# Semaphores of a finished phase cleared one phase later: one barrier between phases in place of two

## The chip, the core and the metric

The kernel runs on one NeuronCore of a Trainium2 chip. The core has five engines that run side by side, each through its own list of instructions: TensorE (PE, with its weight loads as PEld), VectorE (DVE), ScalarE (ACT), GpSimd (POOL) and SyncE (SP, which here only issues DMAs). They are kept in order by semaphores: an instruction adds to one when it ends, another engine waits until it has reached a number. Sixteen DMA engines move data between memory and the core's buffers. The metric is the time of one execution on the device in microseconds; the median of several runs counts.

## The reference

One layer of a hybrid network is computed for 128 context tokens and 512 latent tokens, 640 rows of 1024 numbers:

```python
def layer(x, mod, init_f, init_b, ctx_k, ctx_v, pos, lp):
    shift1, scale1, gate1, shift2, scale2, gate2 = jnp.split(mod, 6, axis=-1)
    h = modulate(rmsnorm(x, lp['norm1_w']), shift1, scale1)
    mix, s_f, s_b, k, v = token_mixer(h, init_f, init_b, ctx_k, ctx_v, pos, lp)
    x = x + gate1 * mix
    h = modulate(rmsnorm(x, lp['norm2_w']), shift2, scale2)
    x = x + gate2 * peer(h, lp['w_pq'], lp['peer_keys'], lp['peer_u'], lp['peer_v'])
    return x, s_f, s_b, k, v
```

token_mixer projects h once, runs a state-space scan in both directions (ssd_scan) and grouped attention beside each other, and merges both with sigmoid gates. peer picks for each token and each of 8 heads the best 16 of 16384 single-neuron experts by two lists of 128 keys, and sums gate * gelu(x.u) * v over them. The change touches none of this arithmetic.

## The kernel before

The work is cut into ten phases that follow each other: modulate, tokens, attention, attn_out, ssd, ssd_out, mix_out, route, gates and experts. `build` (line 2565) calls `run_phase` for each. A phase allocates its buffers and semaphores, and then opens one `nc.Block()` with a function for every engine that has work in it: `block.sync` issues DMAs, `block.tensor`, `block.vector`, `block.scalar` and `block.gpsimd` hold the instructions of the four compute engines. Inside a phase the order is that of the code, engine by engine, with semaphores between them. A block ends with a barrier: every engine drains, reports to POOL and goes on when POOL releases it.

All phases use the same numbers of semaphores again, and each phase counts from zero. So `run_phase` opens a second block behind each phase (lines 2558 to 2562), in which POOL clears that phase's semaphores one by one, and which ends with a barrier of its own. The phases have 36, 40, 19, 6, 48, 21, 16, 25, 8 and 31 semaphores, 250 in all. In the profile line 2562 is the clear, and line 2558 the barrier behind the clears.

Weights come as a stream of units of 1 MB (`Stream`, line 87): SP loads a unit into one of two buffers (`load`, L98), ACT rounds it to its upper part (`hi`, L106), DVE makes the remainder (`lo`, L111), and PE multiplies with both. The stream's semaphores, the two for the gate matrix (`K.g_out`) and the eight for gathered rows (`K.gathered`) belong to no phase and are never cleared. Loads for the first units of a phase are issued in the phase before it; a phase's own parameters are loaded by SP at its start.

Two places matter besides. The gates phase (line 2100) builds a matrix of gate weights and writes it to memory in blocks, the last of them as `g_late` (L2130). The experts phase (line 2194) begins on SP and on POOL with the wait for all of these writes; then SP loads pieces of the matrix (`p_g`, L2247 and L2249), and POOL issues 256 indirect DMAs (L2308) that gather rows of u and v into `p_uv`, while PE, ACT and DVE run all experts over the other tokens. `K.pool_dma_sems` (line 2574) are twelve more semaphores that no instruction uses.

Of the kernel before, what the change touches and what calls it, by code (L numbers as in the profile page):

```python
# [27 lines left out]
NT = T // P  # L28
# [278 lines left out]
def phase_tokens(nc, K, ctx):  # L307

    S = Stream(nc, K)
    sem = K.phase_semaphores(ctx)  # L310
# [53 lines left out]
    with nc.Block() as block:  # L364
# [47 lines left out]
        @block.gpsimd  # L412
        def _(pool):
            nc.gpsimd.memset(b_row[:, :], 0.0).then_inc(brow_zero, 1)
            pool.wait_ge(nrm_in, 48)
            for n, w in enumerate((wq, wk)):
                for f in range(2):
                    part = w[:, :].rearrange("p (a f d) -> p a f d", a=2, f=2)[:, :, f, :].unsqueeze(1).to_broadcast([P, 4, 2, 16])
                    for j in range(2):
                        nc.gpsimd.tensor_tensor(rope[:, n, f, j], cs[:, j, :, :].rearrange("p t (a d) -> p t a d", a=2), part,  # L420
                                                ALU.mult).then_inc(tab_done, 1)

        @block.scalar
        def _(act):
# [249 lines left out]
def phase_attention(nc, K, ctx):  # L674

    S = Stream(nc, K)
    sem = K.phase_semaphores(ctx)
# [52 lines left out]
    with nc.Block() as block:  # L730
# [12 lines left out]
        @block.gpsimd  # L743
        def _(pool):
            nc.gpsimd.memset(cin[:, :, :], 0.0).then_inc(zero, 1)

        @block.tensor
        def _(pe):
# [167 lines left out]
def phase_attn_out(nc, K, ctx):  # L916
    S = Stream(nc, K)
    sem = K.phase_semaphores(ctx)
    sb = lambda n, s, d=F32: ctx.enter_context(nc.sbuf_tensor(n, s, d))
    oT = [sb(f"g_oT{i}", [P, KD, T], F32R) for i in range(2)]  # L920
    yb = [sb(f"g_yb{i}", [P, 4, TH]) for i in range(2)]
    ps = [[ctx.enter_context(nc.psum_tensor(f"g_ps{s}{i}", [P, TH], F32)) for i in range(4)] for s in range(2)]
    oh_done = sem("g_oh"); ol_done = sem("g_ol"); mm_done = sem("g_mm"); ev_done = sem("g_ev")
    out_done = [sem("g_out0"), sem("g_out1")]

    with nc.Block() as block:
        @block.sync
        def _(sp):
            for i in range(N_AT):
                S.load(sp, U_AT + i + 3, (i + 1) % 2)  # L930
                sp.wait_ge(ev_done, 4 * (i + 1))
                sp.dma_start(K.yb_dram[2 * i:2 * i + 2].rearrange("m p t -> p m t"),
                             yb[i % 2][:, :, :].rearrange("p (m a) t -> p m (a t)", a=2)).then_inc(out_done[i % 2], 16)
            for s in range(2):
                sp.wait_ge(out_done[s], 16 * N_AT // 2)

        @block.tensor
        def _(pe):
            for i in range(N_AT):
                s = i % 2  # L940
                S.ready(pe, U_AT + i)
                if i >= 2:
                    pe.wait_ge(ev_done, 4 * (i - 1))
                wh, wl = (x[s][:, :].rearrange("p (k c) -> p k c", k=KD) for x in (K.whi, K.wlo))
                for m in range(2):
                    for k in range(KD):
                        if i == 0 and m == 0 and k % 2 == 0:
                            pe.wait_ge(ol_done, k // 2 + 1)
                        cols = slice(m * P, (m + 1) * P)
                        for lhs, rhs, f, l in ((wh, oT[0], k == 0, False), (wh, oT[1], False, False), (wl, oT[0], False, k == KD - 1)):  # L950
                            for h in range(2):
                                mm = nc.tensor.matmul(ps[s][2 * m + h][:, :], lhs[:, k, cols], rhs[:, k, h * TH:(h + 1) * TH],
                                                      start=f, stop=l)
                mm.then_inc(mm_done, 1)
                pe.drain().then_inc(K.hilo_free, 1)

        @block.scalar
        def _(act):
            for q in range(4):
                nc.scalar.activation(oT[0][:, 2 * q:2 * q + 2, :], K.QT[:, 2 * q:2 * q + 2, :], ACT.Copy).then_inc(oh_done, 1)  # L960
            for i in range(N_AT):
                act.wait_ge(mm_done, i + 1)
                if i >= 2:
                    act.wait_ge(out_done[i % 2], 16)
                for b in range(4):
                    nc.scalar.activation(yb[i % 2][:, b, :], ps[i % 2][b][:, :], ACT.Copy).then_inc(ev_done, 1)
                S.hi(act, U_AT + i + 2, i % 2)

        @block.vector
        def _(dve):  # L970
            for q in range(4):
                dve.wait_ge(oh_done, q + 1)
                nc.vector.tensor_tensor(oT[1][:, 2 * q:2 * q + 2, :], K.QT[:, 2 * q:2 * q + 2, :],
                                        oT[0][:, 2 * q:2 * q + 2, :].bitcast(F32), ALU.subtract).then_inc(ol_done, 1)
            for i in range(N_AT):
                S.lo(dve, U_AT + i + 2, i % 2)
# [4 lines left out]
def phase_ssd(nc, K, ctx):  # L981

    S = Stream(nc, K)
    sem = K.phase_semaphores(ctx)
# [72 lines left out]
    with nc.Block() as block:  # L1057
# [63 lines left out]
        def _(pool):  # L1121
# [45 lines left out]
            for q in range(SLOTQ):  # L1167
                a, b, f = ssd_steps(q)
                g, k = (q - 2) // NT, (q - 2) % NT
                if 0 <= g < GROUPS:  # L1170
                    carry(g, k)
                    if k == 4:
                        carry(g, 5)
                if b is not None:
                    forward_part(b)
                if q >= NT - 1 and q - NT + 1 < STEPS:
                    build_rT(q - NT + 1)
                if b is not None:
                    skip(b)

        @block.tensor
        def _(pe):
# [264 lines left out]
def phase_ssd_out(nc, K, ctx):  # L1447
# [30 lines left out]
    with nc.Block() as block:  # L1478
# [97 lines left out]
        @block.gpsimd  # L1576
        def _(pool):
            pool.wait_ge(row_done, 2)
            for c in range(4):
                pool.wait_ge(sig_done, 2 * c + 2)  # L1580
                nc.gpsimd.tensor_tensor(ga[c % 2][:, :, :], ga[c % 2][:, :, :], rrow[:, :].unsqueeze(1).to_broadcast([P, 2, T]),
                                        ALU.mult).then_inc(scaled, 1)

        @block.scalar
        def _(act):
# [66 lines left out]
def phase_mix_out(nc, K, ctx):  # L1652
# [20 lines left out]
    with nc.Block() as block:  # L1673
        @block.sync
        def _(sp):
            sp.dma_start(x[:, :, :], K.x.rearrange("(t p) d -> p t d", p=P)).then_inc(x_in, 16)
            for g in range(2):
                sp.dma_start(g1[:, g, :], K.gates[g:g + 1, 0:D].partition_broadcast(P).rearrange("p o d -> p (o d)")).then_inc(x_in, 16)
            for n in range(U_O, U_PQ):
                S.load(sp, n + 3, (n + 3) % 2)  # L1680
            for t in range(NT):
                sp.wait_ge(res, NT + t + 1)
                sp.dma_start(K.x2_dram[t * P:(t + 1) * P, :], x[:, t, :]).then_inc(x_out, 16)
                sp.wait_ge(x_out, 16 * (t + 1))

        @block.tensor
        def _(pe):
# [120 lines left out]
def phase_route(nc, K, ctx):  # L1808
# [50 lines left out]
    with nc.Block() as block:  # L1859
# [9 lines left out]
        def _(pool):  # L1869
            for h in range(LOOKED_UP):  # L1870
# [5 lines left out]
                for i, n in enumerate((8 * TOPK, 4 * TOPK, 2 * TOPK)):  # L1876
# [3 lines left out]
                nc.gpsimd.tensor_tensor(slots[:, 0:2, :, TOPK * h:TOPK * (h + 1)], pair[:, :, :, 0:TOPK], pair[:, :, :, TOPK:2 * TOPK],  # L1880
                                        ALU.add).then_inc(x_done, 1)
                pool.wait_ge(x_done, h + 1)

        @block.tensor
        def _(pe):
# [214 lines left out]
def phase_gates(nc, K, ctx):  # L2100
# [20 lines left out]
    with nc.Block() as block:  # L2121
# [23 lines left out]
        @block.gpsimd  # L2145
        def _(pool):
            for g in range(ALL):
                pool.wait_ge(hot_done, 2 * g + 1)
                nc.gpsimd.tensor_tensor(oi[g % HOT][:, :, :], oi[g % HOT][:, :, :],
                                        K.slotsT[:, 2, Q * g:Q * (g + 1)].unsqueeze(2).to_broadcast([P, Q, P]), ALU.mult).then_inc(weighted, 1)  # L2150

        @block.tensor
        def _(pe):
# [40 lines left out]
def phase_experts(nc, K, ctx):  # L2194
# [43 lines left out]
    with nc.Block() as block:  # L2238
# [62 lines left out]
        def _(pool):  # L2301
# [10 lines left out]
            nc.gpsimd.tensor_tensor(ys[:, 0, :], ys[:, 0, :], gate2[:, group(0), :], ALU.mult).then_inc(gated0, 1)  # L2312
            pool.wait_ge(gated0, 1)
            nc.gpsimd.tensor_tensor(res[0], res[0], ys[:, 0, :], ALU.add).then_inc(summed0, 1)

        @block.tensor
        def _(pe):
# [222 lines left out]

def run_phase(nc, K, phase):

    K.sems = []

    def phase_semaphores(ctx):
        def sem(name):
            K.sems.append(ctx.enter_context(nc.semaphore(name)))
            return K.sems[-1]
        return sem

    def pool_dma(i):

        return K.pool_dma_sems[i]

    K.phase_semaphores, K.pool_dma = phase_semaphores, pool_dma
    with ExitStack() as ctx:
        phase(nc, K, ctx)
        with nc.Block() as block:  # L2558
            @block.gpsimd
            def _(pool):  # L2560
                for s in K.sems:
                    pool.sem_clear(s)


def build(nc, K):
    ctx = ExitStack()
    with ctx:
# [3 lines left out]
        K.whi = [sb(f"w_hi{i}", [P, 8 * UC], F32R) for i in range(2)]  # L2571
        K.wlo = [sb(f"w_lo{i}", [P, 8 * UC], F32R) for i in range(2)]
        K.w_loaded = [sem("w_loaded0"), sem("w_loaded1")]
        K.pool_dma_sems = [sem(f"pool_dma{i}") for i in range(NT + 7)]
        K.w_hi_done, K.w_lo_done, K.hilo_free = (sem(n) for n in ("w_hi_done", "w_lo_done", "hilo_free"))
        K.ident, K.ones, K.iota = sb("ident", [P, P]), sb("ones", [P, P]), sb("iota", [P, P])
        K.tri_le, K.tri_gt, K.tri_ge, K.tri_lt = (sb(n, [P, P]) for n in ("tri_le", "tri_gt", "tri_ge", "tri_lt"))
# [29 lines left out]
        with ExitStack() as s:  # L2607
# [4 lines left out]
            for phase in (phase_route, phase_gates):  # L2612
                run_phase(nc, K, phase)
        run_phase(nc, K, phase_experts)


def pack_units(w, cols=UC):
# [71 lines left out]
```

## Time and profile before

| | us |
|---|---|
| median of 3 runs | 2834.81 |
| fastest and slowest run | 2831.0 and 2839.09 |
| span of the profiled execution | 2836.8 |

The page gives one time for the profiled execution, its span from the first instruction to the last; the runs' median is 2.0 us below it. Of the span PE is busy 2575.1 us, DVE 2142.1, ACT 1135.1 and POOL 864.4. Clears, barriers and other semaphore instructions are not counted as busy, so a stretch in which a core only clears semaphores reads as idle on all engines. Names such as POOLq or SPq mean an engine's instruction queue: what it did outside its compute unit. Line numbers are those of the kernel before.

### The profile page before, as it was taken

Reading aid. Unit: us, or ns where it says so; the run is one execution under the profiler, and the core shown is the slowest. Engines: PE = TensorE matmul, PEld = TensorE weight load, DVE = VectorE, ACT = ScalarE, POOL = GpSimd, SP = SyncE. Lnnn points to the kernel's source line nnn. Section 1 sums busy time; section 2 is a strip of 40 time slices with the busy share of each in tenths; the row PEclk is TensorE's granted clock in tenths of the full one; section 3 lists DMA queues with packets and bytes.
Section 4 is the critical chain, followed back from the end, with each engine's and each line's share of the span. In section 5 each row is a group of like instructions: output and inputs, shape, how many; then the busy total and the mean of one; then the engine's idle time right before and its main releaser. Section 6 shows DMA issues by size and latency. Waiting matters only on the chain. (4 is left out here: it accounts for less than half of the span.)

```text
span 2836.8 us, 39212 instructions
## 1 busy us (share of the span) xinstructions
PE 2575.1 (91%) x14998; PEld 2227.3 (79%) x14998; DVE 2142.1 (76%) x3785; ACT 1135.1 (40%) x1882; POOL 864.4 (30%) x623
## 2 busy tenths in 40 slices
PE   5979999978899999698799988899999999999996
PEld 3868777768788787598688668788888888888885
DVE  2646667661478777433489978699999999999998
ACT  3324445442465565332334467233333323333332
POOL 0000000000466666110023356343433443334431
PEclk9989999989999999799799999899999999999998
DMA  5521112122223222342312338999999999999995
GB/s 227 223 110 49 49 64 82 51 95 104 105 75 129 96 80 84 104 178 97 126 51 76 112 115 250 401 417 416 418 414 417 418 413 417 413 412 419 411 410 232
DMA packets 166265, 621.49 MB, mean 219 GB/s; under 512 B 14880, under 2 KB 83264, under 8 KB 105664
## 3 DMA queue, kind: packets, MB, share of 16 engines
q1 hardware_dynamic: 124608, 340.03, 32.2%
q0 software_dynamic: 36864, 268.45, 23.0%
q10 hardware_dynamic: 4608, 10.52, 1.2%
q8 instruction: 119, 1.95, 0.3%
q14 instruction: 66, 0.54, 0.1%
HBM read 559.39 MB, written 59.56 MB: 218 GB/s over the span
## 5 line engine op out<-in xcount | busy, mean ns | idle before, releaser
L2308 POOL DMA_INDIRECT p_uv<-in_uv_rows,merged x256 | 395.6, 1545 | 625.1 <-DVE merged L2475 564.7
L2475 DVE SCALAR_TENSOR_TENSOR merged<-p_uv,p_sw,merged 128x1024 f32<-128x1024 f32 x256 | 330.9, 1292 | 7.5 <-DVE p_sw L2465 0.4
L2328 PE MATMUL p_pa<-h2D,w_hi 128*128 128x384 f32 x896 | 318.2, 355 | 3.0 <-PEq L2558 2.2
L2458 DVE CUSTOM_DVE_ANT_0 p_uv<-p_uv,merged 128x1024 f32<-128x1024 f32 x256 | 308.0, 1219 | 16.7 <-DMA p_uv<-in_uv_rows,merged 16.7
L2330 PE MATMUL p_pa<-h2D,w_lo 128*128 128x384 f32 x896 | 301.9, 337 | 0.0
L2329 PE MATMUL p_pa<-h2D,w_hi 128*128 128x384 f32 x896 | 301.8, 337 | 0.0
L2343 PE MATMUL p_py<-w_hi,p_wh 128*128 128x512 f32 x672 | 267.6, 398 | 15.0 <-DVE w_lo L2429 15.0
L2372 ACT ACTIVATE w_hi<-w_raw 128x2048 fp32r<-128x2048 f32 x110 | 210.4, 1913 | 173.8 <-DMA w_raw<-in_w_stream 88.6
L2429 DVE TENSOR_TENSOR w_lo<-w_raw,w_hi 128x2048 fp32r<-128x2048 f32 x110 | 251.8, 2289 | 22.7 <-ACT w_hi L2372 22.6
L2344 PE MATMUL p_py<-w_lo,p_wh 128*128 128x512 f32 x672 | 266.7, 397 | 0.0
L2345 PE MATMUL p_py<-w_hi,p_wl 128*128 128x512 f32 x672 | 266.7, 397 | 0.0
L111 DVE TENSOR_TENSOR w_lo<-w_raw,w_hi 128x2048 fp32r<-128x2048 f32 x64 | 153.2, 2395 | 102.3 <-ACT w_hi L106 102.3
L1145 POOL TENSOR_TENSOR s_pv<-s_pv,decay 128x256 f32<-128x256 f32 x48 | 41.1, 856 | 536.8 <-ACT s_st L1306 535.6
L801 PE MATMUL c_pp<-hT,w_hi 128*128 128x320 f32 x1024 | 199.1, 317 | 0.0
L2328 PEld LDWEIGHTS p_pa<-h2D,w_hi 128*128 128x128 f32 x896 | 169.0, 189 | 14.0 <-issue 12.0
L2329 PEld LDWEIGHTS p_pa<-h2D,w_hi 128*128 128x128 f32 x896 | 169.1, 189 | 10.0 <-issue 9.6
L2330 PEld LDWEIGHTS p_pa<-h2D,w_lo 128*128 128x128 f32 x896 | 168.9, 189 | 0.0
L106 ACT ACTIVATE w_hi<-w_raw 128x2048 fp32r<-128x2048 f32 x64 | 122.5, 1914 | 112.5 <-PEq L1574 68.5
L2343 PEld LDWEIGHTS p_py<-w_hi,p_wh 128*128 128x128 f32 x672 | 127.0, 189 | 45.9 <-DVE w_lo L2429 17.4
L801 PEld LDWEIGHTS c_pp<-hT,w_hi 128*128 128x128 f32 x1024 | 161.6, 191 | 0.3
L853 DVE TENSOR_REDUCE a_nmax<-a_ps 128x1 f32<-128x640 f32 (+1 forms) x80 | 57.4, 717 | 130.5 <-PE a_ps L759 112.7
L2345 PEld LDWEIGHTS p_py<-w_hi,p_wl 128*128 128x128 f32 x672 | 127.0, 189 | 30.9
(379 smaller groups left out, 6271.5 us busy)
## 6 DMA issues: line engine op xcount, KB each, us to landing
w_raw<-in_w_stream SPq DMA_DIRECT2D x174, 1024.0 KB, 9.1
g_pairs<-e_st SPq DMA_DIRECT2D x5, 4096.0 KB, 16.1
p_g<-g_pairs SPq DMA_DIRECT2D x64, 320.0 KB, 8.4
t_ada<-in_w_ada SPq DMA_DIRECT2D x16, 1024.0 KB, 10.3
xc_dram<-c_xc SPq DMA_DIRECT2D x8, 1284.0 KB, 4.5
p_ve<-in_v_early SPq DMA_DIRECT2D x8, 1024.0 KB, 13.5
r_ur<-in_u_early ACTq DMA_DIRECT2D x14, 512.0 KB, 3.6
s_xx<-xc_dram SPq DMA_DIRECT2D x8, 642.0 KB, 6.0
```

The costliest lines, as they stand in the source:

```text
L801: mm = nc.tensor.matmul(ps_p[:, h, 0:TH], lhs[:, k, cols], rhs[:, k, h * TH:(h + 1) * TH], start=f, stop=l)
L2308: nc.gpsimd.indirect_dma_start(uv[:, k % RING, :], None, K.uv_rows, bass.IndirectOffsetOnAxis(K.sidx[:, t, c:c + 1], 0)).then_inc(K.gather ...
L2328: nc.tensor.matmul(ps_a[m][:, :], wh[:, k, cols], K.h2D[0][:, k, :], start=k == 0, stop=False)
L2329: nc.tensor.matmul(ps_a[m][:, :], wh[:, k, cols], K.h2D[1][:, k, :], start=False, stop=False)
L2330: mm = nc.tensor.matmul(ps_a[m][:, :], wl[:, k, cols], K.h2D[0][:, k, :], start=False, stop=k == KD - 1)
L2343: nc.tensor.matmul(ps_y[o][:, :], Wh[s][:, c, tc], vh[:, c, dc], start=first and c == 0, stop=False)
L2344: nc.tensor.matmul(ps_y[o][:, :], Wh[s][:, c, tc], vl[:, c, dc], start=False, stop=False)
L2345: mm = nc.tensor.matmul(ps_y[o][:, :], Wl[s][:, c, tc], vh[:, c, dc], start=False, stop=last and c == 1)
L2372: nc.scalar.activation(K.whi[slot][:, :], K.raw[slot][:, :], ACT.Copy).then_inc(K.w_hi_done, 1)
L2429: nc.vector.tensor_tensor(K.wlo[slot][:, :], K.raw[slot][:, :], K.whi[slot][:, :].bitcast(F32), ALU.subtract).then_inc(K.w_lo_done, 1)
L2458: nc.vector.tensor_tensor_reduce(uv[:, b, 0:D], uv[:, b, 0:D], K.hrow[:, t, :], 1.0, 0.0, ALU.mult, ALU.add, sa[:, at:at + 1]).then_inc(do ...
L2475: nc.vector.scalar_tensor_tensor(ys[:, t, :], uv[:, b, D:2 * D], sw[:, at:at + 1], ys[:, t, :], ALU.mult, ALU.add).then_inc(v_done, 1)
```

## The change

The clears move into the next phase. `run_phase` no longer opens a block of its own. Every phase ends its POOL function with `K.clear_previous(pool)`, which clears the semaphores of the phase before it; phases that had no POOL function (attn_out, mix_out) get one that holds only this. Since a phase's semaphores now live until the next phase is over, two sets are held at a time, and the numbers of a set are free again for the phase after the next. The twelve unused semaphores are dropped. The last phase's 31 semaphores are not cleared any more.

```diff
@@ phase_tokens, and likewise at the end of POOL's function in attention, ssd, ssd_out, route, gates, experts
                         nc.gpsimd.tensor_tensor(rope[:, n, f, j], cs[:, j, :, :].rearrange("p t (a d) -> p t a d", a=2), part,
                                                 ALU.mult).then_inc(tab_done, 1)
+            K.clear_previous(pool)
@@ phase_attn_out, and likewise mix_out
+        @block.gpsimd
+        def _(pool):
+            K.clear_previous(pool)
@@ run_phase
-    K.sems = []
+    sem_ctx, sems = ExitStack(), []
 
     def phase_semaphores(ctx):
         def sem(name):
-            K.sems.append(ctx.enter_context(nc.semaphore(name)))
-            return K.sems[-1]
+            sems.append(sem_ctx.enter_context(nc.semaphore(name)))
+            return sems[-1]
         return sem
 
-    def pool_dma(i):
-
-        return K.pool_dma_sems[i]
-
-    K.phase_semaphores, K.pool_dma = phase_semaphores, pool_dma
+    def clear_previous(pool):
+
+        for s in K.previous_sems:
+            pool.sem_clear(s)
+
+    K.phase_semaphores, K.clear_previous = phase_semaphores, clear_previous
     with ExitStack() as ctx:
         phase(nc, K, ctx)
-        with nc.Block() as block:
-            @block.gpsimd
-            def _(pool):
-                for s in K.sems:
-                    pool.sem_clear(s)
+    K.previous_ctx.close()
+    K.previous_ctx, K.previous_sems = sem_ctx, sems
@@ build
-        K.pool_dma_sems = [sem(f"pool_dma{i}") for i in range(NT + 7)]
+        K.previous_ctx, K.previous_sems = ExitStack(), []
...
         run_phase(nc, K, phase_experts)
+        K.previous_ctx.close()
```

On POOL at the handover from modulate to tokens (ISA is a clear; the branches open and close blocks; `tri_lt` and `iota` are modulate's last work, `q_brow` and `q_rope` tokens' own) the difference of the two orders reads:

```order
 L189 IOTA iota 128x128
 L160 UNCONDITIONAL_BRANCH
-L2559 UNCONDITIONAL_BRANCH
-L2562 ISA x36
-L2558 UNCONDITIONAL_BRANCH
 L412 UNCONDITIONAL_BRANCH
 L414 MEMSET q_brow 128x512
 L420 TENSOR_TENSOR q_rope<-q_cs,q_w 128x128 x4
 L420 TENSOR_TENSOR q_rope<-q_cs,k_w 128x128 x4
+L2569 ISA x36
 L364 UNCONDITIONAL_BRANCH
```

The 36 clears went from between the two phases to behind tokens' last tensor instruction, and one block with its barrier is gone.

On POOL at the end of the program, before, from the end of the gates phase (`h`) through the experts phase (`p_uv`, `merged`):

```order
L2149 TENSOR_TENSOR h<-h,slotsT 128x1024 x48
L2121 UNCONDITIONAL_BRANCH
L2559 UNCONDITIONAL_BRANCH
L2562 ISA x8
L2558 UNCONDITIONAL_BRANCH
L2300 UNCONDITIONAL_BRANCH
L2308 DMA p_uv<-in_uv_rows,merged 128x2048 x256
L2312 TENSOR_TENSOR merged<-merged,w_raw 128x1024
L2314 TENSOR_TENSOR merged<-merged 128x1024
L2238 UNCONDITIONAL_BRANCH
L2559 UNCONDITIONAL_BRANCH
L2562 ISA x31
```

and of the changed kernel, the same stretch (line numbers are 12 to 14 higher there):

```order
L2162 TENSOR_TENSOR h<-h,slotsT 128x1024 x48
L2569 ISA x25
L2134 UNCONDITIONAL_BRANCH
L2314 UNCONDITIONAL_BRANCH
L2322 DMA p_uv<-in_uv_rows,merged 128x2048 x256
L2326 TENSOR_TENSOR merged<-merged,w_raw 128x1024
L2328 TENSOR_TENSOR merged<-merged 128x1024
L2569 ISA x8
L2252 UNCONDITIONAL_BRANCH
```

The clears of route (25) now stand behind POOL's last work in gates, those of gates (8) behind its last work in experts, and the 31 at the end are gone. On PE, ACT, DVE and SP the order of the instructions is as before but for the second barrier's.

## Rows read from the trace of the kernel before

**Rows 1.** The page's part 1: busy us (share of the span) xinstructions, by engine.

```profile
PE 2575.1 (91%) x14998; PEld 2227.3 (79%) x14998; DVE 2142.1 (76%) x3785; ACT 1135.1 (40%) x1882; POOL 864.4 (30%) x623
```

**Rows 2.** Stretches: us from:to, length, busy us of each engine (xinstructions), PEclk, DMA share, GB/s.

```profile
1770.30:2834.30 1064.00, 1026.37 (x4896) 884.65 (x4896) 1002.66 (x1201) 331.57 (x406) 400.90 (x258) 0.98 0.99 403
```

**Rows 3.** Stretches, same columns: from first clear to release, nine handovers and the end.

```profile
57.00:59.70 2.70, 0.00 (x0) 0.00 (x0) 0.00 (x0) 0.00 (x0) 0.00 (x0) 0.50 0.19 79
191.00:194.10 3.10, 0.00 (x0) 0.00 (x0) 0.00 (x0) 0.00 (x0) 0.00 (x0) 0.50 0.00 0
631.30:632.80 1.50, 0.00 (x0) 0.00 (x0) 0.00 (x0) 0.00 (x0) 0.00 (x0) 0.50 0.00 0
701.70:702.30 0.60, 0.00 (x0) 0.00 (x0) 0.00 (x0) 0.00 (x0) 0.00 (x0) 0.50 0.00 0
1165.00:1168.60 3.60, 0.00 (x0) 0.00 (x0) 0.00 (x0) 0.00 (x0) 0.00 (x0) 0.50 0.00 0
1311.00:1313.00 2.00, 0.00 (x0) 0.00 (x0) 0.00 (x0) 0.00 (x0) 0.00 (x0) 0.50 0.02 4
1404.90:1406.20 1.30, 0.00 (x0) 0.00 (x0) 0.00 (x0) 0.00 (x0) 0.00 (x0) 0.50 0.00 0
1648.20:1650.20 2.00, 0.00 (x0) 0.00 (x0) 0.00 (x0) 0.00 (x0) 0.00 (x0) 0.50 0.00 0
1769.40:1770.20 0.80, 0.00 (x0) 0.00 (x0) 0.00 (x0) 0.00 (x0) 0.00 (x0) 0.50 1.52 655
2834.30:2836.80 2.50, 0.00 (x0) 0.00 (x0) 0.00 (x0) 0.00 (x0) 0.00 (x0) 0.50 0.00 0
```

**Rows 4.** Line 2562, whole span and 1160 to 1200: ns min/median/max, first and last start.

```profile
L2562 POOLq EVENT_SEMAPHORE_RANGE_CLEAR  x250: 44/44/48, 56.9 to 2836.5; - x125
...
L2562 POOLq EVENT_SEMAPHORE_RANGE_CLEAR  x48: 44/44/44, 1165.0 to 1168.3; - x48
```

**Rows 5.** SyncE's waits: who waited for whom, us in total, times, longest.

```profile
SPq L2558 <- PEq L2558: 19.8, 10, 3.6
```

**Rows 6.** Timeline of the first handover: start, us, engine, line, out<-in [idle before <-releaser].

```profile
59.70 0.33 SPq L373 DMA_DIRECT2D dt_bias<-in_dt_bias_f  x1
59.71 0.52 POOL L414 MEMSET q_brow<- 128x512 f32 x1 [56.86 <-POOLq L2558]
59.71 1.28 ACT L450 ACT_TABLE_LOAD   x1 [3.07 <-PEq L2558]
...
59.75 0.77 PE L647 MATMUL t_row<-ident,decay 64*128 64x64 f32 x5 [3.90 <-PEq L2558]
```

**Rows 7.** Timeline of the ninth handover, same columns.

```profile
1774.95 0.33 SPq L2247 DMA_DIRECT2D p_g<-g_pairs  x1
...
1775.80 1.12 POOL L2308 DMA_INDIRECT p_uv<-in_uv_rows,merged  x1 [15.28 <-DMA g_late<-e_st]
```

**Rows 8.** The chain that ended last, same handover: start, us, what.

```profile
1763.78 11.10 DMA g_late<-e_st
```

**Rows 9.** POOL's last work in ssd, ssd_out, gates: ns min/median/max, first and last start.

```profile
L1156 POOL TENSOR_TENSOR s_xd<-s_xb,s_dsk x40: 608/1056/1060, 751.9 to 1156.7; 128x256 f32<-128x256 f32 x40
...
L1581 POOL TENSOR_TENSOR o_ga<-o_ga,o_rrow x4: 3034/4136/4142, 1218.7 to 1295.4; 128x1280 f32<-128x1280 f32 x4
...
L2149 POOL TENSOR_TENSOR h<-h,slotsT x48: 1894/1897/1897, 1651.9 to 1758.6; 128x1024 f32<-128x1024 f32 x48
```

**Rows 10.** Stretches of PE alone: us from:to, length, busy us (x), PEclk, DMA share, GB/s.

```profile
56.80:59.70 2.90, 0.00 (x0) 0.50 0.25 105
59.70:63.60 3.90, 3.85 (x20) 0.50 0.12 19
...
1406.40:1411.90 5.50, 5.50 (x21) 0.50 0.79 291
...
1770.30:1773.60 3.30, 3.30 (x10) 0.50 1.11 477
```

**Rows 11.** The chain that ended last, a wait in the experts phase.

```profile
2291.98 11.72 DMA w_raw<-in_w_stream
```

More of the change, by code:

```diff
@@ L935, in _ @@
                 sp.wait_ge(out_done[s], 16 * N_AT // 2)
+        @block.gpsimd
+        def _(pool):
+            K.clear_previous(pool)
         @block.tensor
@@ L1179, in _ @@
                     skip(b)
+            K.clear_previous(pool)
         @block.tensor
@@ L1582, in _ @@
                                         ALU.mult).then_inc(scaled, 1)
+            K.clear_previous(pool)
         @block.scalar
@@ L1684, in _ @@
                 sp.wait_ge(x_out, 16 * (t + 1))
+        @block.gpsimd
+        def _(pool):
+            K.clear_previous(pool)
         @block.tensor
@@ L1882, in _ @@
                 pool.wait_ge(x_done, h + 1)
+            K.clear_previous(pool)
         @block.tensor
@@ L2150, in _ @@
                                         K.slotsT[:, 2, Q * g:Q * (g + 1)].unsqueeze(2).to_broadcast([P, Q, P]), ALU.mult).then_inc(weighted, 1)
+            K.clear_previous(pool)
         @block.tensor
@@ L2314, in _ @@
             nc.gpsimd.tensor_tensor(res[0], res[0], ys[:, 0, :], ALU.add).then_inc(summed0, 1)
+            K.clear_previous(pool)
         @block.tensor
```

## The prediction, made before the changed kernel ran

> **What bounds the kernel now.** I read the page's head first: TensorE is busy in 91% of a span of 2836.8 us [rows 1], so no engine has much to give back and a saving must come from time in which all wait. The stretches of time show where that is. From 1770.30 to 2834.30 the experts phase runs with the DMA engines at 0.99 busy and 403 GB/s [rows 2]: it is bound by its transfers, with DVE and PE close behind. Between any two phases stands a stretch in which no compute engine does anything [rows 3]. Its reader should see three things there: PE, DVE, ACT and POOL all at 0.00, their lengths from 0.60 to 3.60 us, and the DMA share: 0.00 to 0.02 in seven of the eight handovers up to the gates phase, 0.19 in the first, 1.52 in the ninth, and 0.00 after the last phase. Where even the DMA engines stand still, nothing that is under way can hide what is taken away.
>
> What fills these stretches is POOL's 250 semaphore clears [rows 4], and SyncE's own waits put the time beside them: ten waits for the barrier after the clears, 19.8 us together, 3.6 us the longest [rows 5].
>
> **What the change takes away.** A handover is now: first barrier, n clears on POOL, second barrier. 48 clears start between 1165.0 and 1168.3 us, which is 3.3 us over 47 steps, 70 ns a clear (each is listed with 44 ns of its own) [rows 4]. The clears go by phase 36, 40, 19, 6, 48, 21, 16, 25, 8 and 31.
> - The first eight handovers hold 211 clears: 211 x 0.070 = 14.8 us. Their stretches in [rows 3] add up to 2.70 + 3.10 + 1.50 + 0.60 + 3.60 + 2.00 + 1.30 + 2.00 = 16.8 us. The difference of 2.0 us over eight is 0.25 us, the second barrier. This whole 16.8 us leaves the path: everything behind it (SyncE's parameter loads, the first matmuls, ACT's first instructions) is released by that barrier, as the first handover shows: SyncE, POOL, ACT and PE all start between 59.70 and 59.75 [rows 6]. SyncE's ten waits give 0.3 us less than the ten stretches (19.8 against 20.1), so I take 16.6.
> - The first handover has DMA at 0.19, a 1 MB load of weights under way. Its first user in the tokens phase comes behind parameter loads which SyncE issues only after the barrier, so nothing waits for that load there either; the 2.70 us count in full. Were it the load that decided, the loss would be at most these 2.70 us.
> - The end of the program: 31 clears and the last barrier, 2.50 us [rows 3], behind the last output's landing. Nothing covers them; they go in full. This counts on the device's time including them, as the span does, and the median within 2 us of the span says that it does; if not, the 2.5 us are missing from the gain.
> - The ninth handover, gates to experts, gives nothing, and here I leave the stretch's 0.80 us out. Both SyncE and POOL open the experts phase by waiting for all writes of the gate matrix. The last one, g_late, is issued at 1763.78 and lands 11.10 us later [rows 8], at 1774.88; SyncE's next load stands at 1774.95 and the first indirect gather at 1775.80 [rows 7]. The release at 1770.2 is 4.7 us earlier than that. PE's first matmuls come 0.8 us sooner and then wait for the same data. Bounds: 0 and 0.80.
>
> **What it adds and moves.** The clears run on POOL behind its last work of the next phase, 219 of them. Wherever they stand between POOL's last result and the phase's barrier, they cost nothing as long as POOL is not the last engine in. The tightest places: ssd, last POOL work starts at 1156.7 and takes at most 1.06, then 6 x 0.07 = 0.4 us, ready at 1158.2 against 1165.0; ssd_out, last start 1295.4 plus at most 4.14, then 48 x 0.07 = 3.4, ready at 1302.9 against 1311.0; gates, last start 1758.6 plus 1.90, then 25 x 0.07 = 1.8, ready at 1762.3 against 1769.4 [rows 3, 4, 9]. Each has some 7 us or more left. In tokens, attention and route POOL's own part is over long before the phase is, and in attn_out and mix_out it has none. In experts the 8 clears, 0.6 us, follow an addition (line 2314) without which DVE can't finish the first output tile; that tile's normalization and its write-out come after, and the clears lie beside them. So this part costs 0. No DMA, no wait and no other instruction is moved on SyncE, ACT, DVE or PE, and the twelve semaphores that are dropped were used by no instruction.
>
> **TensorE's clock.** The handovers are also where the granted clock is at its lower level (0.50 is 1.2 GHz of 2.4). After the first handover PE works from 59.70 to 63.60 at 0.50; after the seventh from 1406.40 to 1411.90; after the ninth from 1770.30 to 1773.60 [rows 10]. A shorter gap shifts these stretches against PE's work and may shorten or lengthen them. Bounds: at best the 3.90 us after the first handover, where PE's gap shrinks from 3.90 us (its idle time in [rows 6]) to 1.2, run at full clock, worth half, 1.95 us. At worst the first and the ninth, each grown to the longest seen, 5.50: (1.6 + 2.2) / 2 = 1.9 us lost. The middle is 0, and I take that.
>
> The Trainium skill, page "TensorE: Matmul & The Clock Gate", section "HAM oscillation — how this bites in real kernels", says that long gaps between bursts of matmuls re-throttle the engine, each at a price. The trace agrees in that all ten rows of the idle stretches have the clock at 0.50. By that rule a gap made short enough keeps its clock; this is the first rival below.
>
> **Sum.** 16.6 + 2.5 = 19.1 us. On the profiled execution, whose span is its time on the device here, 2836.8 - 19.1 = 2817.7. The median of the runs is 2834.81, 2.0 below, inside their spread of 2831.0 to 2839.09. So the forecast is 2834.81 - 19.1 = 2815.7. Two kernels of this length are told apart from about 0.3%, 8.5 us: faster means below 2826.3.
>
> **Rivals.**
> 1. *The clock stays up at the first handover.* For it: PE's gap there shrinks by more than two thirds. Against it: the clock stood at 0.50 from 56.80 on [rows 10], 1 us behind PE's last matmul (it ended at 59.75 - 3.90 = 55.85 [rows 6]), so before the first clear. Time 2815.7 - 1.95 = 2813.8. Chance 0.08.
> 2. *The jump into the next phase stops being free.* Today every engine but POOL has up to 3.6 us of waiting before it starts the next phase; if fetching the new phase's instructions takes as long as that, taking the wait away uncovers it. The inner 16.6 us come back and only the end's 2.5 stay: 2832.3. Against it: POOL itself passes the second barrier within about 0.3 us of its last clear and starts its memset at 59.71 [rows 6], though it had no wait to hide a fetch in. Chance 0.06. The Trainium skill, page "Runtime: NRT & Kernel Launch", section "Instruction fetch mechanics", says that a taken branch to a far target stalls for a fetch; no run here shows such a stall, and the trace speaks against it at POOL.
> 3. *Part of the gain is given back inside phases*, by loads that the stand-still had let run ahead. The handovers with DMA at 0.00 leave no room for it; half of the inner 16.6 as a bound gives 2824.0. Chance 0.08.
> 4. *Slower.* The experts phase has its transfers at 0.99. PE enters it 0.8 us earlier against the gathers than now. In one of its cycles the chain that ended last stood 11.72 us on the landing of a weight load, from 2291.98 [rows 11]. If the new start makes such waits come more often, each costs 11.7 us; two use up the 19.1, from there on it is slower. With three: 2815.7 + 35.2 = 2850.9. For it: that phase is 1064 us, the longest, with every unit near its limit. Against it: the bytes to move are the same, and the gathers, weights and gate tiles start at the same landing of g_late as before. Chance 0.06.
> 5. *The change does not do what it says*, because POOL comes last somewhere and its clears stay on the path. The margins above of some 7 us exclude it but for a rest that I put into the range.
>
> **The numbers.** Forecast 0.72, rivals as given. Range 2807 to 2825: the forecast with the bounds of the clock (-1.95, +1.9) and of the ninth handover (-0.8), the first handover's 2.7 and some 4 us for the median of few runs that spread over 8; it takes in the rivals 1 and 3. Faster by over 0.3%: 0.72 + 0.08 + most of rival 3 = 0.86. Within 0.3%: rival 2 and the rest of 3, 0.09. Slower: 0.05, most of rival 4.
>
> **What would show it.** In the new profile the gap between the last work of a phase and the first of the next shrinks by each stretch of [rows 3]; 219 clears instead of 250, none of them in a stretch where all engines are idle; nothing on POOL's clears in anybody's wait; the experts phase, from its first gather to the last output, as long as before within 2 us, and the first gather still 12 us behind the issue of g_late; the program ending within 0.3 us of the last barrier's release. Wrong would be: engines idle for over 0.5 us behind the one barrier that is left (rival 2), or an experts phase that is longer by ten microseconds or more (rival 4).

## The result, and the profile after

The changed kernel takes 2812.03 us in the median of four runs (2809.52 to 2818.15); the kernel before, measured beside it four times, 2834.7. The ratio is 0.9922, 95% interval [0.991, 0.9934]: 22 us faster, between 19 and 26. Five more runs of it on another occasion gave 2818.83 and 0.9941 [0.9928, 0.9955]. The nine together have a mean of 2815.6; 32 runs of the kernel before that ran beside the experiments have 2834.5. So the change is worth about 19 us, give or take 3 (an estimate from the scatter of these runs); the forecast was 19.1 and 2815.7.

The page of the changed kernel, its head (span, then busy us, share and instructions of each engine):

```profile
span 2807.9 us, 39070 instructions
...
PE 2568.6 (91%) x14998; PEld 2223.7 (79%) x14998; DVE 2142.4 (76%) x3785; ACT 1136.1 (40%) x1882; POOL 865.3 (31%) x623
```

The work is the same; what goes is idle time. These are the nine handovers now, as stretches from the release of the one barrier to the first instruction behind it, rounded (us from:to, length, busy us of PE, PEld, DVE, ACT, POOL, PEclk, DMA share, GB/s):

```profile
54.00:54.10 0.10, 0.00 (x0) 0.00 (x0) 0.00 (x0) 0.00 (x0) 0.00 (x0) 0.50 0.02 0
185.50:185.55 0.05, 0.00 (x0) 0.00 (x1) 0.00 (x0) 0.00 (x0) 0.01 (x1) 0.50 0.00 0
622.20:622.30 0.10, 0.00 (x0) 0.00 (x0) 0.00 (x0) 0.00 (x0) 0.00 (x0) 0.50 0.00 0
690.30:690.36 0.06, 0.00 (x0) 0.00 (x0) 0.00 (x0) 0.00 (x0) 0.00 (x0) 0.50 0.00 0
1149.40:1149.50 0.10, 0.00 (x0) 0.00 (x0) 0.00 (x0) 0.00 (x0) 0.00 (x0) 0.50 0.00 0
1289.10:1289.18 0.08, 0.00 (x0) 0.00 (x0) 0.00 (x0) 0.00 (x0) 0.00 (x0) 0.50 0.00 0
1381.70:1381.75 0.05, 0.00 (x0) 0.00 (x0) 0.00 (x0) 0.00 (x0) 0.00 (x0) 0.50 0.00 0
1623.20:1623.30 0.10, 0.00 (x0) 0.00 (x0) 0.00 (x0) 0.00 (x1) 0.00 (x0) 0.50 0.00 0
1741.90:1742.00 0.10, 0.00 (x0) 0.00 (x1) 0.00 (x0) 0.00 (x0) 0.00 (x0) 0.50 0.00 0
```

They answer to [rows 3]: 0.07 to 0.10 us by the trace's own start times, where 0.60 to 3.60 stood. Measured the same way in both traces, from the end of the first barrier to the first instruction of the next phase, the nine take 18.8 us before and 0.7 after. The last stretch of [rows 3], 2.50 us behind the last output, is 0.1. The timeline of the first handover, which answers to [rows 6], shows SyncE, ACT, POOL and PE off at once 0.1 us behind the release at 54.0 (DVE has no work there yet):

```profile
54.10 0.33 SPq L373 DMA_DIRECT2D dt_bias<-in_dt_bias_f  x1
54.10 1.28 ACT L451 ACT_TABLE_LOAD   x1 [0.26 <-PEq L160]
54.11 0.53 POOL L414 MEMSET q_brow<- 128x512 f32 x1 [51.25 <-POOLq L160]
54.15 0.76 PE L648 MATMUL t_row<-ident,decay 64*128 64x64 f32 x5 [1.09 <-PEq L160]
```

PE's idle time in the last row is 1.09 us, where [rows 6] has 3.90.

The two spans differ by 28.9 us, which is more than the change does. 18.1 of it are the handovers, 2.4 the end; the other 8.4 lie inside phases whose code is the same, 2.8 in modulate, 3.6 in ssd and 2.7 in ssd_out above all. The experiments had to say whether the change makes those shorter.

### The profile page after: what moved, and what is told of

It is laid out like the page before. It is cut to its first block and busy times, and to the rows that moved or that the text cites. A ratio compares the mean times of both kernels' runs of the same rounds, so it can differ in the third digit from the quotient of the medians.

```text
span 2807.9 us, 39070 instructions
## 1 busy us (share of the span) xinstructions
PE 2568.6 (91%) x14998; PEld 2223.7 (79%) x14998; DVE 2142.4 (76%) x3785; ACT 1136.1 (40%) x1882; POOL 865.3 (31%) x623
## 5 line engine op out<-in xcount | busy, mean ns | idle before, releaser
L2358 PEld LDWEIGHTS p_py<-w_hi,p_wh 128*128 128x128 f32 x672 | 126.6, 188 | 44.2 <-DVE w_lo L2444 15.8
L2394 ACT ACTIVATE p_a<-p_pa 128x384 f32<-128x384 f32 x112 | 54.7, 489 | 248.3 <-PE p_pa L2345 248.3
```

The lines of the kernel that those rows point to most:

```text
L2358: nc.tensor.matmul(ps_y[o][:, :], Wh[s][:, c, tc], vh[:, c, dc], start=first and c == 0, stop=False)
```

## The experiments

Every kernel ran against the kernel before in five or more runs. A ratio is to the kernel before; the changed kernel stands at 19 us below it. "By the traces" means the lengths of the stretches that the edit touches, read from one profiled execution of each kernel.

**The changed kernel again**, unaltered.

> The changed kernel, unaltered, in five rounds against the kernel before. Theory (the ten stand-stills of 20.1 us are removed, the ninth's 0.8 us comes back as a longer wait for the gate matrix): 19 to 20 us faster. Rival (the change also moves TensorE's clock or the start-up loads to the better): 22 us or more, with phases other than the handovers shorter in the trace, and shorter by the same amounts as in the first trace (modulate by 2.8 us, ssd by 3.6, ssd_out by 2.7). If those phase differences do not come back, they are the scatter of single executions.

Measured: 0.9941 [0.9928, 0.9955], 16.7 us faster, between 13 and 20, which holds the theory's 19 to 20 and not the rival's 22. The handovers take 0.7 us again, and the phase differences do not come back. The next experiment shows why.

**The kernel before again**, unaltered.

> The kernel before, unaltered, for a second trace of it. Theory (handovers are fixed, phases scatter by 1 to 4 us from one execution to the next): handovers of 18.8 us and an end of 2.5 us again, while modulate, ssd and ssd_out are up to 3 us shorter than in the first trace. Rival (the changed kernel has shorter phases by its own doing): the same 56.8, 462.6 and 142.3 us as in the first trace.

Measured: 1.0001 [0.9991, 1.0011]. Its nine handovers take 18.8 us, the end 2.5 and SyncE's ten waits 19.8, as before. The stretches of four phases (modulate, ssd, ssd_out, experts; columns as above) are, in this second trace of the kernel before:

```profile
0.00:54.00 54.00, 25.90 (x220) 18.89 (x220) 17.82 (x32) 26.90 (x45) 2.00 (x12) 0.92 0.68 264
701.15:1160.40 459.25, 409.73 (x2552) 351.42 (x2552) 335.24 (x473) 255.92 (x618) 277.04 (x256) 0.95 0.28 92
1164.10:1303.70 139.60, 126.68 (x860) 124.19 (x860) 52.89 (x67) 44.72 (x58) 15.46 (x4) 0.96 0.45 155
1762.50:2827.40 1064.90, 1026.90 (x4896) 885.49 (x4896) 1002.41 (x1201) 331.95 (x406) 400.91 (x258) 0.98 0.99 403
```

the first three of them in the first trace of the kernel before (experts is in [rows 2]):

```profile
0.00:56.80 56.80, 25.30 (x220) 17.23 (x220) 17.83 (x32) 26.56 (x45) 2.01 (x12) 0.94 0.65 249
702.39:1165.00 462.61, 413.88 (x2552) 354.18 (x2552) 335.09 (x473) 255.70 (x618) 276.86 (x256) 0.94 0.28 92
1168.69:1311.00 142.31, 129.23 (x860) 126.61 (x860) 52.89 (x67) 44.73 (x58) 15.45 (x4) 0.94 0.44 152
```

in the first trace of the changed kernel:

```profile
0.00:54.00 54.00, 26.04 (x220) 18.70 (x220) 17.82 (x32) 26.78 (x45) 2.02 (x12) 0.91 0.68 267
690.35:1149.40 459.05, 410.23 (x2552) 352.06 (x2552) 335.26 (x473) 255.86 (x618) 277.20 (x256) 0.95 0.28 93
1149.50:1289.10 139.60, 126.63 (x860) 124.16 (x860) 52.90 (x67) 44.73 (x58) 15.47 (x4) 0.96 0.44 155
1742.00:2807.80 1065.80, 1027.39 (x4896) 886.36 (x4896) 1002.74 (x1201) 332.45 (x406) 401.36 (x258) 0.98 0.99 403
```

and in its second:

```profile
0.00:56.70 56.70, 25.34 (x220) 17.21 (x220) 17.82 (x32) 26.57 (x45) 2.00 (x12) 0.94 0.64 250
692.15:1155.00 462.85, 414.71 (x2552) 355.10 (x2552) 334.90 (x473) 255.85 (x618) 277.28 (x256) 0.94 0.28 92
1155.07:1297.20 142.13, 129.22 (x860) 126.59 (x860) 52.90 (x67) 44.72 (x58) 15.47 (x4) 0.94 0.43 152
1750.95:2817.00 1066.05, 1027.25 (x4896) 885.95 (x4896) 1002.37 (x1201) 331.77 (x406) 401.97 (x258) 0.98 0.99 403
```

Either kernel has a trace with 54.0, 459 and 139.6 us, and one with 57, 463 and 142. So these are differences between single executions and not the change. Nor do the three go together: "Only the end removed" has 53.4, 465.0 and 139.7 us, "Clears by range" 56.7, 460.5 and 142.1. In ssd and ssd_out the longer form has PE busy 2.5 to 5 us more at a mean clock of 0.94, where the shorter has 0.95 and 0.96. The rival of this experiment is refuted; that the first pair of traces set a long form against a short one in all three was chance.

**Only the end removed.**

```diff
     with ExitStack() as ctx:
         phase(nc, K, ctx)
+        if phase is phase_experts:
+            return
         with nc.Block() as block:
```

> The kernel before, without the clears and the barrier behind the last phase only. Theory: 31 clears of 70 ns and one barrier of 0.25 us, 2.5 us faster (ratio 0.9991). Rival (the measured time ends at the last output's landing, or the device clears anyway): 0.

Measured: 0.9994 [0.9985, 1.0003], 1.7 us faster; the interval holds both 0 and 2.5, so the times alone do not decide. The traces do: the execution ends with the one barrier behind the last output, and an execution's own time is 1.77 us above its span here, 1.78 in the kernel before and 1.76 in the changed kernel. The device's time follows the span, and the span contains the end's clears, so the end counts. What resets these 31 semaphores for the next execution, when the kernel no longer does, no run looks at.

**An empty second block** behind every phase of the changed kernel.

```diff
         phase(nc, K, ctx)
+        if True:
+            with nc.Block() as block:
+                @block.gpsimd
+                def _(pool):
+                    pass
     K.previous_ctx.close()
```

> The changed kernel with an empty second block behind every phase: the clears stay hidden, the second barrier is back, ten times. Theory (a barrier is 0.25 us, a clear 70 ns): 2.3 us slower than the changed kernel, 17 us faster than before. Rival (the barrier itself, with every engine draining and branching, is what costs, 2 us each): near the kernel before, 0 to 2 us faster.

Measured: 0.9956 [0.9942, 0.9969], 12.5 us faster than before, between 9 and 16. The rival's 0 to 2 lie far outside, and the theory's 17 just outside too, though the traces alone would give 16.6. The nine handovers add up to 3.8 us, 3.1 more than in the changed kernel (0.32 to 0.34 in eight of them, 0.41 in the sixth), and the end has a stretch of 0.40. The barrier is a small part of the 20 us, as the theory has it. In an empty block it is a third larger than the 0.25 I had derived, because POOL finds nothing to do and has to wait until the others have drained: at the second handover POOL drains at 186.76 us, PE, the last of them, at 186.88. Behind clears the others have long drained (in [rows 6]'s handover by 57.0, the last clear starts at 59.35), and there 0.25 holds; the 64 clears further down confirm it. SyncE's waits (in total, times, longest) for the second barrier:

```profile
SPq L2575 <- PEq L2575: 2.7, 10, 0.3
```

**Every semaphore cleared twice** in the kernel before.

```diff
                 for s in K.sems:
                     pool.sem_clear(s)
+                    pool.sem_clear(s)
```

> The kernel before with every semaphore cleared twice in the second block. Theory (each clear between two barriers costs its 70 ns in full, but for those behind the gates phase): 242 x 0.070 = 16.9 us slower than before (ratio 1.006), and the handover from gates to experts longer by 0.6 us with an experts phase that is shorter by as much. Rival (clears overlap with something, or a part of the time is given back): half of it, 8 us.

Measured: 1.0074 [1.006, 1.0088], 21 us slower, between 17 and 25; the theory's 16.9 is at the lower end, the rival's 8 outside. The same wait as above, [rows 5] being that of the kernel before:

```profile
SPq L2558 <- PEq L2558: 38.2, 10, 7.3
```

It grows from 19.8 to 38.2, 18.4 us for 250 clears, 74 ns each, and the longest is 7.3 where 3.6 stood. Each clear between two barriers is paid in full. The 74 are 71 ns from one clear to the next, in both kernels, and three pauses of POOL's queue of 0.3 to 0.4 us in these handovers, where the kernel before has one (at 1312.2 us). The small side forecast, an experts phase 0.6 us shorter, failed: it took 1067.1 us from its first instruction on, 3.0 more than in the first trace of the kernel before. g_late needed 12.06 us to land there, 1.0 more than in the other traces, and that phase scatters from 1064.1 to 1066.1 in the four traces of unaltered kernels; the rest is open.

**Clears by range** in the kernel before.

```diff
-                for s in K.sems:
-                    pool.sem_clear(s)
+                nums = sorted(s.num for s in K.sems)
+                first = last = nums[0]
+                for n in nums[1:] + [None]:
+                    if n == last + 1:
+                        last = n
+                        continue
+                    pool.sem_clear(range(first, last + 1))
+                    first = last = n
```

> The kernel before, both barriers kept, but POOL clears a phase's semaphores by ranges of adjacent numbers, 15 instructions in place of 250. Theory (the clears cost 73 ns each by count, whatever range one covers, and a barrier 0.33 us): 235 clears fewer, of which 7 behind the gates phase count for nothing: 228 x 0.073 = 16.7 us faster than before. Rival (a clear costs by the semaphores in it): 0.

Measured: 0.9954 [0.9941, 0.9967], 13 us faster, between 9 and 17, which barely holds the theory's 16.7 and excludes the rival's 0; the traces have 15.8 less in the handovers and the end together, 15.3 without the ninth. The clears of all phases, and those of the handover behind ssd with its 48 semaphores (ns min/median/max, first and last start):

```profile
L2567 POOLq EVENT_SEMAPHORE_RANGE_CLEAR  x15: 64/91/244, 56.7 to 2821.0; - x15
...
L2567 POOLq EVENT_SEMAPHORE_RANGE_CLEAR  x2: 88/166/243, 1158.1 to 1158.2; - x2
```

and SyncE's wait for the second barrier:

```profile
SPq L2558 <- PEq L2558: 4.0, 10, 0.6
```

One clear of many semaphores takes up to 244 ns where one of a single semaphore takes 44, so both forecasts were too simple: there is a price by the number covered. It is small: a clear of 6 semaphores took 67 ns, of 19 135, of 36 228 and of 40 244, some 5 ns for each further one. The 48 semaphores go in two instructions, and the longest wait falls from 3.6 to 0.6 us. Two barriers with ranges come within some 6 us of the changed kernel without a second live set: 4.8 us of handovers and 0.7 at the end, against 0.7 and 0.1, 4.7 us by the traces.

**The same delay in two places** of the changed kernel, once behind ssd and once behind gates.

```diff
         phase(nc, K, ctx)
+        if phase is phase_ssd:          # in the other kernel: phase_gates
+            with nc.Block() as block:
+                @block.gpsimd
+                def _(pool):
+                    for _i in range(64):
+                        pool.sem_clear(K.pad)
     K.previous_ctx.close()
...
+        K.pad = sem("pad")
```

Behind ssd:

> The changed kernel with a second block of 64 clears of one unused semaphore between ssd and ssd_out. Theory (nothing is under way in that handover, the stand-still counts in full): 64 x 0.073 + 0.33 = 5.0 us slower than the changed kernel. Rival (later waits take it up): less than 2.

Measured: 0.9947 [0.9934, 0.9961], 15 us faster than before, 3.9 less than the changed kernel's 18.9. In the trace the handover is 4.86 us, from 1150.89 to 1155.75, 4.78 more than in the changed kernel: 64 steps of 71 ns and 0.25 us for the barrier. The phase behind it is no shorter than in the other traces (141.7 us, against 139.6 and 142.2):

```profile
L2579 POOLq EVENT_SEMAPHORE_RANGE_CLEAR  x64: 44/44/44, 1150.9 to 1155.4; - x64
```

Behind gates:

> The changed kernel with the same block of 64 clears between gates and experts. Theory (the experts phase opens by waiting 6.0 us for g_late, and 5.0 us fit under that wait): 0 us slower, SyncE's wait for g_late down from 6.0 to 1.0, first gather still 12.0 us behind the issue of g_late. Rival (the first matmuls of the experts phase decide, not the gate matrix): 5.0 us slower as in the fifth handover.

Measured: 0.9923 [0.9907, 0.9939], 22 us faster than before, between 17 and 26. The rival's 14 us lie outside, though not by much: the six runs scatter over 14 us. The clears stand at the same kind of place for the same time,

```profile
L2579 POOLq EVENT_SEMAPHORE_RANGE_CLEAR  x64: 44/44/44, 1751.2 to 1755.6; - x64
```

and SyncE's wait for g_late at the start of experts is down to

```profile
SPq L2276 <- DMA g_late<-e_st: 1.4, 1, 1.4
```

from 6.0 us in the changed kernel (1.0 was forecast); the first gather stands 12.16 us behind the issue of g_late, where 12.0 was forecast. Measured from that gather, PE's first matmul of the phase comes 4.6 us later than in the changed kernel, its 100th of 4896 at 26.0 us against 25.7 and 25.1 in the two traces, its 500th at 115.3 against 114.4 and 115.3. So the wait paid for the delay within the first matmuls, and the handover behind gates is worth nothing. One thing stays open: this trace, of the slowest of the six runs, takes 1062.2 us from the first gather to the barrier behind the last output, where eight other traces take 1058.4 to 1059.4 and that of the doubled clears 1061.0. The 3 us arise later (the 4000th matmul at 854.3 against 851.0 and 851.4), and nothing here ties them to the delay or excludes it.

## Why the prediction was right

**The stand-stills.** For the first eight handovers I took 16.6 us. The traces have 17.8 before and 0.6 after, 17.2. The parts are 211 clears of 71 ns, 14.9 us, eight barriers of 0.25 us, 2.0, and one pause of 0.3 us between two clears of ssd_out. So the price of a clear and that of a barrier stood, and the missing 0.6 come from how I read the stretches: those of [rows 3] begin or end up to 0.2 us inside the handover (the first at 57.00, where the barrier's release came at 56.83), which makes 0.4, and the 0.2 that I took off for SyncE's waits should have stayed, since SyncE's wait begins only 0.1 us behind the release, when it has drained. The end gave 2.4 us for 2.5. The two errors are small and go the same way.

**The first handover's load.** I counted its 2.70 us in full though a load was under way. The tokens phase behind it took 131.3 and 132.4 us in the kernel before and 131.4 and 130.0 in the changed one, so no loss shows there.

**Nothing is given back by loads (rival 3).** The 64 clears behind ssd cost 4.8 us in their handover, and the total moved by 3.9 with an interval of about 4 either way. In the trace they are paid in full; by the times a fraction could still be given back.

**The ninth handover.** Predicted 0 of its 0.80 us. In the changed kernel the first gather (start, us, line, out<-in [idle before]) stands where the landing of g_late puts it, the chain's row first:

```profile
1736.81 11.08 DMA g_late<-e_st
```

```profile
1748.81 1.12 POOL L2322 DMA_INDIRECT p_uv<-in_uv_rows,merged  x1 [15.24 <-DMA g_late<-e_st]
```

That is 12.00 us behind the issue, as the 12.02 of [rows 7, 8]; SyncE waits for the landing:

```profile
SPq L2276 <- DMA g_late<-e_st: 6.0, 1, 6.0
```

where it waited 4.7 us before. The padded kernel settled it from the other side.

**POOL's clears behind its last work.** They cost nothing, in nobody's wait, but I had them in the wrong place. I let them start when POOL's last result was ready. In the trace the six clears in ssd start here (the second fence has POOL's last two operations there):

```profile
L2569 POOLq EVENT_SEMAPHORE_RANGE_CLEAR  x6: 44/44/44, 1139.6 to 1139.9; - x6
```

```profile
1139.60 1.54 POOL L1170 TENSOR_TENSOR s_A<-s_stl,dt 128x512 f32<-128x512 f32 x1 [4.54 <-DVE s_stu L1400]
1141.10 0.61 POOL L1162 TENSOR_TENSOR s_xd<-s_xb,s_dsk 128x256 f32<-128x256 f32 x1
```

The first clear starts 0.04 us before the first of the two operations, and the last is over when the second has yet to begin, 9.5 us before the barrier; POOL's drain, which follows the clears, then lasts from 1139.99 until the second operation has ended, at 1141.78. The margin was larger than the sum had it in ssd (9.5 us for 6.8), in ssd_out (12.3 for 8.1) and in gates (8.1 for 7.1).

**The clock (rival 1)** did not stay up, though PE's gap fell to 1.09 us. PE's stretches behind the first and the seventh handover, in the first trace of the changed kernel (us from:to, length, busy, PEclk, DMA share, GB/s):

```profile
54.15:58.10 3.95, 3.95 (x20) 0.50 0.13 23
...
1381.70:1385.00 3.30, 3.21 (x12) 0.50 0.68 204
```

Behind the first, PE runs for 3.95 us at 0.50, as for 3.90 in [rows 10]. But in this trace the clock was low already before the gap; the fair test is the second trace of the changed kernel. PE's last stretches before the gap and behind it, in the first (two lines) and the second:

```profile
51.40:53.10 1.70, 1.65 (x6) 0.50 0.77 299
54.15:58.10 3.95, 3.95 (x20) 0.50 0.13 23
...
53.10:55.70 2.60, 1.06 (x6) 1.00 0.50 126
56.80:60.10 3.30, 3.28 (x17) 0.50 0.32 105
```

There the clock was at 1.00 up to the gap and at 0.50 behind it, for 3.3 us; in the two kernels with the delay, whose first handover is the changed kernel's, it was at 0.50 for 6.2 and 3.4 us of PE's work there. So rival 1 is refuted. Two more things offset each other. PE's time at 0.50 from its first matmul behind the seventh handover fell from 5.5 and 4.9 us in the two traces of the kernel before to 4.2 and 3.5, and the same behind the ninth grew from 3.5 and 3.3 to 5.7 and 5.5, where the wait for g_late covers it. Over all nine handovers these stretches add up to 51.0 and 42.4 us before, 45.3 and 51.8 in the changed kernel: the clock's term of 0 held within that scatter. The Trainium skill's page "TensorE: Matmul & The Clock Gate" ("HAM oscillation — how this bites in real kernels") makes the gap the cause; here the gap shrank by 2.8 us and a low stretch of 3.3 to 4.0 us behind it remained.

**The jump (rival 2)** is free: SyncE starts 0.07 to 0.08 us behind the release in seven of the nine handovers and PE 0.12 us in five, with nothing between the release and that instruction in which a fetch could hide; elsewhere they have data to wait for. The stall at a far branch, which the Trainium skill's page "Runtime: NRT & Kernel Launch" ("Instruction fetch mechanics") describes, shows in no handover.

**The experts phase (rival 4)** took 1065.8 and 1066.1 us in the changed kernel, 1064.1 and 1064.9 in the one before. Of the difference of 1.4, 0.8 is the ninth handover's time coming back. The remaining 0.6 is within what four traces can tell; from the first gather on it is 1059.0 and 1059.3 us against 1058.5 and 1059.4. A single further wait of 11.7 us would have shown.

**The median.** The forecast of 2815.7 rests on the profiled execution's being 2.0 us from the median. It was one of the slower ones: an execution takes 1.8 us more than its span, so 2836.8 stands for some 2838.6, an estimate. The first comparison's 22 us lie 3 above the forecast, the second's 16.7 lie 2 below, and the nine runs together are at it. That they meet it to 0.1 us is luck, since their mean is itself known to some 3 us; what the traces bear out is the sum, 17.2 us for eight handovers, 0 for the ninth and 2.4 for the end, together 19.7 before rounding, where 19.1 was forecast.

## What to carry to other kernels

Where a kernel clears semaphores one by one between two barriers, every engine pays for each clear, here 71 ns times 250, 17.7 of the 20.5 us of standing still that left the trace; look for stretches in which all engines read 0.00 at once, since bookkeeping is not counted as busy. Such a stretch counts in full only if nothing else is under way: read the DMA share in it, and what the first instructions behind it wait for. If a second live set is not to be had, clearing by ranges gets most of the gain. And one trace against another can be out by 8 us in phases that did not change, so take the size of a small gain from stretches that the change touches, and the total from many runs.

## What the runs showed of the hardware beside

- A clear of one semaphore is listed with 44 ns and comes every 71 ns; one of a range took 64 to 244 ns.
- Between clears POOL's queue pauses now and then for 0.3 us. The pause stands at the same instruction in both traces of the kernel before, behind the 580th that the trace lists of POOL, and with doubled clears behind the 68th and the 964th: they lie multiples of 128 instructions apart. The cause is open.
- A block's drain and barrier with nothing in it costs 0.33 us from release to release, and behind clears 0.25; then 0.07 to 0.10 us pass between release and first instruction.
- POOL's queue executes semaphore clears ahead of tensor operations that stand before them in its program and are not yet computed, as in ssd above. Here the semaphores belong to the phase before. No run clears one that such an operation still uses; that this would be a race is inferred from the order seen.
